# A transformer layer on one NeuronCore: three steps of stick-breaking attention change places

## The reference

```python
z = jnp.einsum('bqhd,bkhd->bhqk', q[:, start:end], k[:, :end]) * (HEAD_DIM ** -0.5)
log_1mb = jnp.where(strict, jax.nn.log_sigmoid(-z), 0.0)
log_w = jax.nn.log_sigmoid(z) + lax.cumsum(log_1mb, axis=3, reverse=True) - log_1mb
wts = jnp.where(strict, jnp.exp(log_w), 0.0)
outs.append(jnp.einsum('bhqk,bkhd->bqhd', wts, v[:, :end]))
```

## Time and profile before

| | |
|---|---|
| median of 3 runs | 1457.89 us (1455.29 to 1458.75) |
| the profiled execution's own time | 1458.07 us |
| its span in the profile | 1456.3 us |
| PE busy | 1417.5 us, 97% |
| DVE busy | 1213.7 us, 83% |
| ACT busy | 971.5 us, 67% |
| POOL busy | 498.7 us, 34% |

### The profile page before, as it was taken

One profiled execution on the slowest core, in us unless ns is written; L12 is line 12 of the kernel. 1 busy time (PEld: TensorE's weight loads), 2 busy tenths in 40 slices (PEclk: granted clock), 3 DMA queues, 4 the chain that ended last, 5 costly groups with the idle time before them and its releaser, 6 DMA issues.

```text
span 1456.3 us, 20301 instructions
## 1 busy us (share of the span) xinstructions
PE 1417.5 (97%) x6451; PEld 1087.6 (75%) x6451; DVE 1213.7 (83%) x1001; ACT 971.5 (67%) x703; POOL 498.7 (34%) x318
## 2 busy tenths in 40 slices
PE   6999989999999999999999999999999999999996
PEld 3465554688888888888888888888888888888873
DVE  5633348599999999999999999999999999999985
ACT  2245660267777777777777777777777777777772
POOL 4400025143344333344444343343333333334001
PEclk9999999999999999999999999999999999999998
DMA  7221127569999999999999999999999999999943
GB/s 256 84 62 54 44 90 279 188 282 377 378 378 374 377 381 382 389 381 374 390 379 381 377 384 384 387 388 382 380 375 378 381 375 381 377 383 376 358 140 129
DMA packets 85741, 459.32 MB, mean 315 GB/s; under 512 B 11852, under 2 KB 26450, under 8 KB 36562
## 3 DMA queue, kind: packets, MB, share of 16 engines
q1 hardware_dynamic: 75198, 431.92, 75.4%
q0 software_dynamic: 9072, 24.39, 7.2%
q10 hardware_dynamic: 1444, 2.66, 0.7%
HBM read 443.92 MB, written 23.66 MB: 321 GB/s over the span
## 4 chain that ended last, share of the span: by engine, by line
PE 78%; DVE 1%; DVEq 0%; issue 0%; ACT 0%; ACTq 0%
PE banks L1808 72%; PE banks L1777 2%; PE banks L1783 2%; PE banks L1844 1%; PE banks L1912 0%; PE banks L1790 0%; PE banks L1917 0%; DVE raw L1742 0%; PE banks L1771 0%; DVE glu_lin L1608 0%; DVE raw L1738 0%; DVEq L1612 0%; ACT hi L1389 0%; DVE glu_lin L1614 0%; ACT raw L1473 0%
## 5 line engine op out<-in xcount | busy, mean ns | idle before, releaser
L1573 DVE TENSOR_TENSOR lo<-raw,hi 128x2048 fp32r<-128x2048 f32 x383 | 863.5, 2288 | 68.4 <-ACT hi L1389 66.6
L1389 ACT ACTIVATE hi<-raw 128x2048 fp32r<-128x2048 f32 x382 | 729.6, 1919 | 243.3 <-PE banks L1808 243.3
L1808 PE MATMUL banks<-hi,x_hi 128*128 128x512 f32 x1040 | 285.2, 395 | 2.8 <-DVE glu_lin L1608 1.5
L1808 PE MATMUL banks<-lo,x_hi 128*128 128x512 f32 x1040 | 278.9, 389 | 0.0
L1808 PE MATMUL banks<-hi,x_lo 128*128 128x512 f32 x1040 | 278.8, 389 | 0.0
L1493 POOL TENSOR_SCALAR sel<-cst,rank_e 128x128 bf16<-128x128 f32 x120 | 209.6, 1758 | 135.9 <-issue 135.9
L1808 PEld LDWEIGHTS banks<-lo,x_hi 128*128 128x128 f32 x1040 | 195.3, 188 | 41.2
L1808 PEld LDWEIGHTS banks<-hi,x_lo 128*128 128x128 f32 x1040 | 195.3, 188 | 41.1
L1808 PEld LDWEIGHTS banks<-hi,x_hi 128*128 128x128 f32 x1040 | 190.4, 188 | 39.8 <-issue 3.5
L1513 POOL DMA_INDIRECT acc_dram<-ye,dst_row x31 | 50.0, 1612 | 363.8 <-ACT ye L1410 363.8
L1808 PE MATMUL banks<-hi,a_hi 128*128 128x512 f32 x496 | 156.2, 396 | 0.0
(11 more groups left out here) (279 smaller groups left out, 1191.3 us busy)
## 6 DMA issues: line engine op xcount, KB each, us to landing
raw<-in_w_exp_in SPq DMA_DIRECT2D x256, 1024.0 KB, 7.7
raw<-in_w_exp_out SPq DMA_DIRECT2D x128, 1024.0 KB, 7.2
raw<-in_w_in SPq DMA_DIRECT2D x9, 1024.0 KB, 7.7
raw<-in_w_out SPq DMA_DIRECT2D x4, 1024.0 KB, 5.0
x<-in_x SPq DMA_DIRECT2D x4, 512.0 KB, 6.0
h_dram<-x SPq DMA_DIRECT2D x4, 512.0 KB, 3.9
bias_in<-bias_dram SPq DMA_DIRECT2D x128, 3.0 KB
raw<-acc_dram SPq DMA_DIRECT2D x4, 512.0 KB, 5.2
```

What stands on the lines that cost most here:

```text
L1389: act.activation(hi[:, c0 % PARTS, :], raw[:, ring_slot(c0), :], ACT.Copy).then_inc(hi_done, 1)
L1573: dve.tensor_tensor(lo[:, c0 % PARTS, :], raw[:, ring_slot(c0), :], w_hi.bitcast(F32), ALU.subtract).then_inc(lo_done, 1)
L1808: last = pe.matmul(psum[:, bank + n, :], s[:, k, :], w[:, at:at + 512], start=(first and m == 0 and new), stop=(closes and m == steps - 1 ...
```

## The change

Three things are done. In `STEPS` the logits of heads 1, 2 and 3 go ahead of the values of heads 0, 1 and 2. On ACT the absolute value and its exponential come first, and the copy of the logits to `z` comes behind them, after a wait for the former head's values (`even_done` counts heads 0 and 2, `av_ready` heads 1 and 3); the wait for `w_ready` goes. On DVE the four scans move from step ("lru", 1) to behind head 1's subtraction.

```diff
-         + [("z", 0)] + jobs("bv0") + [("lru", 0)] + jobs("bv1") + [("s", 0)] + jobs("sq0") + [("a", 0)]
-         + [("z", 1)] + jobs("sq1", "sk") + [("lru", 1), ("s", 1)] + jobs("sv") + [("a", 1)]
-         + [("z", 2)] + jobs("g0", "w0", "w1", "w2", "w3") + [("window", 0), ("s", 2)] + jobs("g1", "g2") + [("a", 2)]
-         + [("z", 3)] + jobs("g3", "t0", "t1", "t2", "t3") + [("lru", 2), ("squares", 0), ("s", 3)]
+         + [("z", 0)] + jobs("bv0") + [("lru", 0)] + jobs("bv1") + [("s", 0)] + jobs("sq0") + [("z", 1)]
+         + [("a", 0)] + jobs("sq1", "sk") + [("lru", 1), ("s", 1)] + jobs("sv") + [("z", 2)]
+         + [("a", 1)] + jobs("g0", "w0", "w1", "w2", "w3") + [("window", 0), ("s", 2)] + jobs("g1", "g2") + [("z", 3)]
+         + [("a", 2)] + jobs("g3", "t0", "t1", "t2", "t3") + [("lru", 2), ("squares", 0), ("s", 3)]
...
                         if n:
                             act.wait_ge(sums_used, n)
-                            act.wait_ge(w_ready, n)
-                        for dst, fn in ((z, ACT.Copy), (lg, ACT.Abs)):
+
+                        def from_psum(dst, fn):
                             act.activation(dst[:, 0:512], psum[:, 4, :], fn)
                             act.activation(dst[:, 512:KALL].rearrange("p (b s) -> p b s", b=2),
                                            psum[:, 5:7, 0:384], fn)
+
+                        from_psum(lg, ACT.Abs)
                         act.drain()
-
                         act.activation(lg, lg, ACT.Exp, scale=-1.0)
+                        if n % 2:
+                            act.wait_ge(even_done, n // 2 + 1)
+                        elif n:
+                            act.wait_ge(av_ready, n // 2)
+                        from_psum(z, ACT.Copy)
                         act.drain()
                         act.activation(lg, lg, ACT.Ln, bias=1.0).then_inc(z_logs, 1)
...
                         dve.tensor_tensor(z2, z2, psum[:, 5:7, 0:384], ALU.subtract).then_inc(sums_used, 1)
+                        if n == 1:
+                            dve.drain()
+                            for c in range(LRU_TILES):
+                                dve.tensor_tensor_scan(xc[:, c, :], t_a[:, c, :], t_x[:, c, :], 0.0, ALU.mult, ALU.add)
...
                             dve.tensor_tensor(t_x[:, c, :], t_x[:, c, :], conv_in[:, c, 0:SEQ], ALU.mult)
-                        dve.drain()
-                        for c in range(LRU_TILES):
-                            dve.tensor_tensor_scan(xc[:, c, :], t_a[:, c, :], t_x[:, c, :], 0.0, ALU.mult, ALU.add)
...
-                    if h % 2:
-                        last.then_inc(av_ready, 1)
+                    last.then_inc(av_ready if h % 2 else even_done, 1)
```

More of the change, by code:

```diff
@@ L360, in hybrid_layer @@
         w_exp, w_ready = sem("w_exp"), sem("w_ready")
-        av_ready, av_copied = sem("av_ready"), sem("av_copied")
+        av_ready, av_copied, even_done = sem("av_ready"), sem("av_copied"), sem("even_done")
         kdup_ready, vshift_ready = sem("kdup_ready"), sem("vshift_ready")
```

## The result

The changed kernel takes 1451.26 us (median of 5 runs, 1450.91 to 1451.68); the kernel before took 1458.75 us in the same comparison (5 runs, 1455.29 to 1460.58). The ratio is 0.995, with a 95% interval of 0.9939 to 0.9962. That is faster by more than 0.3%. The profiled execution after took 1451.68 us with a span of 1450.0 us, against 1458.07 and 1456.3 before: 6.4 us less, where the medians differ by 7.5.

The account below looks back on a forecast made before the run. PE was taken to bound the kernel, with holes ahead of q2. Removing waits gains 8.32 us, less 1.68 for DVE meeting POOL: 6.64 us, from 1458.07 to 1451.4 us, range 1449.0 to 1454.4.

Parts of the forecast that it names:

- head 0's values: PE's wait for POOL's select ahead of head 0's values goes: 0.93 us gained.
- head 1's values: PE's wait ahead of head 1's values goes, and their slowness (3.69 instead of 2.16 us) with it: 4.24 us gained.
- head 2's values: PE's wait for POOL's select ahead of head 2's values goes: 1.64 us gained.
- t3 and DVE's step z of head 3, net: PE's wait ahead of transposes t3 shrinks, at most 1.90 us; DVE's meeting with POOL takes back 1.68; net -0.17.
- head 3's sums: On PE, they start at 188.55 instead of 195.19 us, and all behind moves along: 6.64 us gained.
- The order on PE: The next head's logits, 2.16 us, stand in place of each wait for values; by PE alone 8.71 us with t3.
- DVE against POOL: DVE's step z of head 3 meets the end of POOL's expert bias split; 1.68 us given back, between 0 and 2.1.
- The scans: Behind head 1's subtraction they start it 0.93 us earlier; they stretch to some 5.5 us, POOL's select ends near 142.1.
- The rule of turns: DVE's and POOL's instructions each wait for the other's; each of four select instructions may let a scan of 1.14 us pass.
- Rival 3: Slow clock moves to q1 and head 3's values, 1.5 us lost: 5.1 us gained, 1453.0 us; chance 0.15.

Follow-up runs that it names:

- the order alone: The changed kernel with the scans put back ahead of head 1's subtraction: 1452.61 us, ratio 0.9958 to the kernel before.
- the shorter: The changed kernel without the last TENSOR_TENSOR and CAST of POOL's first bias split: 1450.94 us, ratio 0.9946 to the kernel before.
- the earlier split: The changed kernel with bias loads and the first three instructions of POOL's first bias split moved to the window's exponentials, the rest behind head 2's select: 1450.70 us.
- the late pair: The changed kernel with the last TENSOR_TENSOR and CAST of POOL's first bias split held until DVE's multiplies of lru 2 are done: 1451.28 us, one execution.
- the filled kernel before: The kernel before with products of constants in PE's holes, ten ahead of head 1's values and nine ahead of q1: 1457.29 us, ratio 0.9994.
- the scans alone: The kernel before with only the four scans moved behind head 1's subtraction: 1454.42 us, ratio 0.9973.
- ACT's old order: The changed kernel with ACT's wait and copy of the logits again ahead of the absolute value, Exp and Ln: 1452.35 us, ratio 0.9956.
- the filled earlier split: The changed kernel with POOL's first bias split started earlier and nine products of constants in PE's hole ahead of q1: 1448.89 us, run again 1449.97 us.
- the changed kernel with the filling: The changed kernel with PE's hole ahead of q1 filled with products of constants: 1451.19 us, ratio 0.9952 to the kernel before.

## Why the prediction was right

In distances from the first logits, term by term:

| term | predicted | measured |
|---|---|---|
| head 0's values | 0.93 | 0.95 |
| head 1's values | 4.24 | 4.19 |
| head 2's values | 1.64 | 1.64 |
| t3 and DVE's step z of head 3, net | -0.17 | -0.20 |
| head 3's sums | 6.64 | 6.58 |

(Measured: the start of sq1, g0, g3 and head 3's sums, each less the mark: 32.99 to 32.04, 67.16 to 62.02, 101.63 to 94.85, 112.16 to 105.58.) Behind it, head 3's sums to q2 took 20.02 us against 20.00, and q2 to the first expert's product 83.86 in both: the rest moved as a whole, as said.

**The order on PE** was the carrying step, and the run with the order alone confirms it. That the logits cost nothing new because they stand in the place of the wait is seen in the timeline, where all four groups around them start back to back.

**DVE against POOL.** The row at 27 us and L788 had shown that DVE's operations with two inputs and POOL's wait for each other; L801 was expected at about 2.6 us and took 2.73, the masks ended at 188.64 against 188.5. The runs with the shorter and the earlier split measured the term: 1.87 and 1.85 us, where I took 1.68. So without the meeting the order would have given 8.45 us, where I had 8.32: the two sizes are off by 0.1 to 0.2 in opposite directions, and the net of -0.20 against -0.17 looks more exact than its parts. The working had a slip as well: by its rows the CAST ends at 186.9 + 1.03 = 187.9, and the four masks behind it (0.94) at 188.9, not at 188.5. In the trace the first mask waited while the CAST ran, and the last ended at 188.64.

**The scans.** I expected each of the select's four instructions to let a scan pass and both sides to stretch. The select did (3.71 us, ending at 141.49, against the 142.1 foreseen), but the scans only went from 4.57 to 4.66 us, not to 5.5. The margin of 1.5 us to the logits' end was better than the 0.8 foreseen. The rule of turns that I took from other rows did not hold here: only POOL was held up. Behind the new order the move of the scans is worth 0.6 us, less than its place in the argument suggests.

**The clock.** Rival 3 did not come in the changed kernel's two profiled executions, where q1 ran at full clock, but it came in five variants of it, at the price of 1.7 us (21.7 against 20.0 us from head 3's sums to q2), near the 1.5 foreseen. So the 0.15 that I gave it was low for this family of kernels. The new hole ahead of head 3's sums, which I had named as a part of the case, is not what brings it: three of the five (the shorter and the earlier split, the late pair) do not have that hole. The median of the changed kernel agrees with the sum; that before's median of 1458.75 stands 0.7 above its profiled execution is scatter of before, which I had counted only in the range. That the median came within 0.1 us is luck: the runs of either kernel scatter by more than that, and the start of the program moves by 1.5 us between profiles.

The record also has the mean granted clock of each timed execution. It is 0.997 in the four profiles that have no slow stretch between 60 and 330 us, and 0.994 to 0.996 in the nine others. Of the changed kernel's ten timed executions four had 0.995, which points to a slow stretch that no profile shows, and they took no longer than the rest (1451.14 to 1451.67 us). Of the 35 executions of the kernel before that ran beside the experiments only two had 0.997, and they took 1455.36 and 1455.56 us. Against these two the changed kernel's six with 0.997 (1450.91 to 1451.68) are 3.7 to 4.7 us shorter. This suggests that a good part of the 7.5 us between the medians is clock that the kernel before loses in nearly every execution. It is not shown: these are two executions, on another chip, and none of them was profiled.

The head 1 term holds 1.39 us of clock, measured alone in the run with the filled kernel before. The same amount can be lost again in other places, so a term that is clock is less certain to be kept than one that is waiting.

## What to carry to other kernels

Where a product waits for a long chain over three other engines, put ahead of it the next independent product whose inputs are ready, and check which later consumer holds its buffer: here only the copy into `z` had to wait, and it could stand behind the exponential. Before an engine's step is moved earlier, look at what the neighbouring engine does at its new time: DVE's operation with two inputs from SBUF and POOL's TENSOR_TENSOR and CAST waited for each other, which took 1.9 of 8.4 us. Judge small gains on PE by a distance between two marks in the trace as well as by the median, since the clock can take back 1 to 2 us elsewhere, and compare executions whose mean granted clock is the same.

## What the runs showed of the hardware

- DVE and POOL took turns where DVE read two operands from SBUF (L801 at 2.73 us instead of 1.49, CAST at 2.11 instead of 1.03), and DVE and the CAST did not where one of the two was in PSUM (0.69 and 0.95 us, CAST 1.03). Beside the four scans only POOL lost: 3.71 us for the select instead of 1.02, 4.66 for the scans instead of 4.57. The same lengths to 0.01 us stand in the profiles of the scans alone, ACT's old order, the earlier split and the late pair.
- In four of the thirteen profiles (the changed kernel's two, the scans alone, the first of the filled earlier split) PE's clock stayed at 2.4 GHz from 60 to 330 us. In the others it fell to 1.2 GHz at one or two of three places: behind the hole ahead of head 1's values in the kernel before (idle 2.55 us, cost 1.4), behind the hole ahead of q1 (idle 2.29 us each time; full clock in four profiles, slow in five; cost 1.7), and between 271 and 283 us, in the router, where PE was busy for all of the stretches shown (3.00 of 3.00 us, with small products), at a cost of 0.8 to 1.5 us. Filling a hole kept the clock there in all four executions profiled with it, but in three of these four it then fell in the third place; without a filling it fell there in one profile of nine (the earlier split). What decides between the places stays open.
- The first logits start at 81.6 to 83.1 us after the span's start, in kernels that are the same up to there. Most of the difference lies in the first sixteen 128x512 products, which start at 18.3 to 18.7 us: they took 8.31 us in the kernel before, 8.14 in the changed kernel and 7.03 in the changed kernel with the filling, though the clock shown there is 1.00 in all of them. No experiment was made on it, and the cause is open.
